# Two seven-product steps in each of four pairs of up chunks of a fused two-block transformer kernel

## The chip, the cores and the metric

The kernel runs on one core of a Trainium2 chip. The metric is the device time of one execution in microseconds, the median of the runs shown. Engines are named as the profile does: PE (matrix products; PEld its weight loads), DVE (VectorE), ACT (ScalarE), POOL (GpSimd), SP (SyncE, which issues the loads of the weights).

## What is computed

Two transformer blocks follow each other on 256 tokens of width 2048, in float32. The part that matters here is the feed-forward network of the second block:

```python
h = rmsnorm_2(x, g_ffn[l])
u = causal_dwconv(h @ w_up[l], ffn_conv_w[l]) + ffn_conv_b[l]
gate, val = jnp.split(u, 2, axis=-1)
x = x + (jax.nn.silu(gate) * val) @ w_down[l]
```

`w_up` is 2048 x 11264: the *second up product*. Its result goes through a causal convolution of three taps along the tokens, then SiLU and a product, and becomes the operand of the down product.

## The kernel before

**Granules.** Every weight matrix streams through the core once, as granules of 512 KB: two tiles of 128 rows by 512 columns (one granule is [128, 1024]). SP loads a granule into one of four `raw` slots (`load_granule`, L869). ACT rounds it to `wh` (L938), DVE subtracts `wl = raw - wh` (L1296, "the remainder"), and PE multiplies: for two tiles and two halves of the tokens the three products x_hi*w_hi, x_hi*w_lo and x_lo*w_hi, 12 matmuls of 512 columns (L1882). `wh` and `wl` have four slots too: ACT rounds granule i once PE is done with granule i-4, and SP loads granule i once the remainder of i-4 is taken.

**Chunks.** 512 output columns are a chunk: eight granules for an operand of 2048 rows, gathered in two PSUM banks (256 tokens are two banks). The second up product has 22 chunks, 0 to 21, and 176 granules. Chunks 0 and 1 are interleaved; the others follow each other, in banks 0-1 and 2-3 in turn.

**The order of work.** A plan is made first: a list of rows, one row per granule. Row s holds granule s's rounding and remainder, the load of granule s+4, whatever was booked for row s with `later(row, ...)`, and PE's multiplication of granule s-3. Each engine walks this one list in order and takes its own entries; semaphores tie them together. So a late entry holds up all that stands behind it on its engine.

**What follows an up chunk.** `plan_up(n)` (L537) is called at row s = last granule + 4 (plus a lateness of 0, 4 and 2 rows for chunks 0, 1 and 2), and books:

| row | entry | engine, line |
|---|---|---|
| s | `up_rows`: scale the two banks into `ST` | ACT L1216, L1217 |
| s+1 | `turn`: transpose in 32x32 blocks; `leave`: write to DRAM | DVE L1413, L1415; POOL L1830 |
| s+3 | `bring`: four reads back | POOL L1838 |
| s+9 | `up_keep` | ACT L1224, L1225 |
| s+10 | `up_first`: first tap, four pieces | ACT L1232 |
| s+11 | `up_second`: four pieces, each after its piece of `up_first` | DVE L1743 |
| s+12 | `up_third` | DVE L1750, L1753 |
| s+13 | `up_silu` | ACT L1236 |
| s+14 | `up_gated`, then `act2_hi` | DVE L1757, ACT L1240 |
| s+15 | `act2_lo` | DVE L1761 |

`up_first` of a chunk waits for `act2_lo` of the one before. The banks of a chunk are free for the chunk after next once `up_rows` has read them.

**Seven-product steps.** The first up product ("gated": chunk pairs 1 to 10) and the first chunks of the two down products hold some steps by Strassen's scheme (in Winograd's form). There two chunks run side by side (`product_side_by_side`, L323): granules of both alternate, and two granules of the same weight rows (one for each chunk) make a *unit*, a 2x2 block of tiles against a 2x2 block of the operand. It takes 7 x 3 = 21 matmuls in place of 24: `multiply_base` (9) and `multiply_forms` (12). Four shared banks, those that the chunks themselves do not use, gather the products that go into several outputs. In row u+1 of a unit u stand:

```python
do("base_hi", s - 1)
do("sums", s - 1)
do("base_lo", s - 1)
do("forms_hi", s - 1)
do("forms_lo", s - 1)
```

`base_hi` is ACT L958, `sums` DVE L1324, L1327, L1329, `base_lo` DVE L1310 (it frees both raw slots), `forms_hi` ACT L964, `forms_lo` DVE L1333. PE's two entries stand in row u+4. The first `multiply_base` of a pair waits until the banks that become the shared ones are drained. Five rows after the last unit `shared_out` copies the shared banks out (ACT L980, four copies), then `shared_sums` (DVE L1369, L1371) and `shared_last` (DVE L1376, L1378) in a row each; `shared_bank` (DVE L1399, L1400 for the first chunk of a pair, L1404 for the second) adds them onto the chunk's banks. Sums of the operand that units need are made once per stage (`xs_sum`, `xs_hi`, `xs_lo`).

In the gated stage a pair's two units are its fourth and sixth step, and what follows a pair is little: one transposition for two chunks and no convolution. The second up product has no unit.

Of the kernel before, what the change touches and what calls it, by code (L numbers as in the profile page):

```python
# [8 lines left out]
P = 128  # L9
# [11 lines left out]
ALU = mybir.AluOpType  # L21
# [76 lines left out]
def two_block_kernel(nc, t, out):  # L98
    with ExitStack() as ctx:
# [127 lines left out]
        tile_sums = tmp.rearrange("p (k c) -> p k c", k=4)  # L227
# [4 lines left out]
        xs_in, gated_in = (view(n, [P, 2, 4, P], o) for n, o in (("xs_in", o_a), ("gated_in", o_b + 32 * K)))  # L232
        xs_out, gated_out = (view(n, [P, 2, 4, P], o) for n, o in (("xs_out", o_a + 4 * K), ("gated_out", o_b + 36 * K)))
# [45 lines left out]
        seven_operand = {"gated": "ffn", "out1": "act1", "down": "act2"}  # L279
        side_by_side = {"gated": {}, "out1": {}, "down": {}}  # L280
# [7 lines left out]
        def do(name, *args):  # L288
            plan[-1].append((name, args))
# [193 lines left out]
        def plan_gated(n):  # L483
            def after(s, chunk):
                chunk.drained = [("silu", n), ("gated", n)]
                if n // 2 in GATED_PAIRS:
                    do("shared_bank", n)
# [12 lines left out]
            return after  # L500
# [178 lines left out]
        for n in range(2, 22):  # L679
            last_up = product(t["w_up2"], "N", "ffn2", PAIRS16, ("up", n), plan_up(n), n)  # L680
# [79 lines left out]
        def gated_at(n):  # L760

            return at("shared_bank", n) if n // 2 in GATED_PAIRS else product_of("gated", n)
# [54 lines left out]
        bases = {"gated": (gated_hi, gated_lo), "out1": (base_hi, base_lo), "down": (base_hi, base_lo)}  # L817
        x_places = {"gated": (gated_in, gated_out), "out1": (xs_in, xs_out), "down": (xs_in, xs_out)}
# [98 lines left out]
        def scalar(e):  # L917
# [8 lines left out]
            for name, args in phases:  # L926
# [32 lines left out]
                elif name == "forms_hi":  # L959
# [3 lines left out]
                    e.wait_ge(*at("sums", i))  # L963
                    e.copy(two_slots(wh, i), tile_sums.rearrange("p k c -> p (k c)")).then_inc(done[name], 1)  # L964
                elif name == "xs_hi":
                    stage, j = args
                    e.wait_ge(*at("xs_sum", stage, j))
                    if stage == "gated":
                        e.copy(gated_xs_hi[:], gated_out[:]).then_inc(done[name], 1)
                        continue  # L970
                    e.copy(seven_tiles(operands[seven_operand[stage]][0], stage, j)[:, :, 1], xs_out[:, :, 0])
                    e.copy(xs_hi[:, 2 * j:2 * j + 2], xs_out[:, :, 1:4]).then_inc(done[name], 1)
                elif name == "shared_out":
# [5 lines left out]
                    for k, place in enumerate((0, 3, 2, 1)):  # L979
                        e.copy(tile_sums[:, place, :], ps[:, pair.shared + k, :]).then_inc(done[name], 1)  # L980
# [228 lines left out]
                elif name == "up_rows":  # L1209
# [5 lines left out]
                    e.wait_ge(*product_of("up", n))  # L1215
# [51 lines left out]
        def vector(e):  # L1267
# [22 lines left out]
            for name, args in phases:  # L1290
# [20 lines left out]
                elif name == "sums":  # L1311
                    i, = args
                    unit = seven[i]
                    b12, b11, b22, b21 = (two_slots(raw, i)[:, 512 * k:512 * k + 512] for k in range(4))
# [15 lines left out]
                elif name == "forms_lo":  # L1330
                    i, = args
                    e.wait_ge(*at("forms_hi", i))
                    e.tensor_tensor(two_slots(wl, i), tile_sums.rearrange("p k c -> p (k c)"), two_slots(wh, i).bitcast(F32),  # L1333
                                    ALU.subtract).then_inc(done[name], 1)
                elif name == "xs_sum":
# [3 lines left out]
                    if j > 0:  # L1339
                        e.wait_ge(*at("xs_lo", stage, j - 1))  # L1340
                    elif stage != "gated":

                        e.wait_ge(*through(last_ffn if stage == "out1" else last_up))
# [9 lines left out]
                elif name == "xs_lo":  # L1353
                    stage, j = args
                    e.wait_ge(*at("xs_hi", stage, j))
                    if stage == "gated":
                        e.tensor_tensor(gated_xs_lo[:], gated_out[:], gated_xs_hi[:].bitcast(F32),
                                        ALU.subtract).then_inc(done[name], 1)
                        continue
                    hi, lo = (seven_tiles(x, stage, j)[:, :, 1] for x in operands[seven_operand[stage]])  # L1360
# [3 lines left out]
                elif name == "shared_sums":  # L1364

                    stage, q = args
                    p1, p7, p6, _ = (tile_sums[:, k, :] for k in range(4))
# [4 lines left out]
                elif name == "shared_last":  # L1372
                    stage, q = args
                    _, second, first, p5 = (tile_sums[:, k, :] for k in range(4))
# [4 lines left out]
                elif name == "shared_first":  # L1379
# [5 lines left out]
                    e.tensor_tensor(X[:, 0, n0], X[:, 0, n0], tile_sums[:, 0, :], ALU.add)  # L1385
                    e.tensor_tensor(X[:, 1, n0], X[:, 1, n0], tile_sums[:, 1, :], ALU.subtract).then_inc(done[name], 1)
                elif name == "shared_second":
# [4 lines left out]
                    e.tensor_tensor(X[:, :, n1], X[:, :, n1], tile_sums[:, 2:4, :], ALU.add).then_inc(done[name], 1)  # L1392
                elif name == "shared_bank":
                    n, = args
                    bank0, bank1 = banks(named["gated", n])
                    e.wait_ge(*product_of("gated", n))
                    if n % 2 == 0:
                        e.wait_ge(*at("shared_sums", "gated", n // 2))
                        e.tensor_tensor(bank0, bank0, tile_sums[:, 0, :], ALU.add)  # L1399
                        e.tensor_tensor(bank1, bank1, tile_sums[:, 1, :], ALU.subtract).then_inc(done[name], 1)  # L1400
                    else:
                        b = named["gated", n].bank
                        e.wait_ge(*at("shared_last", "gated", n // 2))
# [786 lines left out]
```

## Time and profile before

| | |
|---|---|
| time, median of 3 runs | 2405.98 us (2405.49 to 2408.77) |
| time of the profiled execution | 2406.82 us |
| its span | 2404.6 us |
| PE busy | 2392.5 us (99%) |
| DVE busy | 1749.4 us (73%) |
| ACT busy | 1351.1 us (56%) |
| DMA, mean | 229 GB/s |
| granted TensorE clock | 0.999 of full |

The span is that of the traced instructions; the time also has what lies before and after them. The profile gives for each group of instructions its busy time and the mean length of one; a timeline gives start and length of single ones, and in brackets how long the engine stood idle before it and whose end released it. Two instructions on one engine overlap by some 0.1 us at their ends, so the distance between their starts is what one costs its engine, and the length is what one waiting for it sees.

### The profile page before, as it was taken

The page shows a single profiled execution, that of the slowest core. Times are in us where ns is not written, and L with a number is a line of the kernel's source. Part 1 is how long each engine was busy: PE and PEld are TensorE (multiplying, and loading weights), DVE is VectorE, ACT ScalarE, POOL GpSimd, SP SyncE. Part 2 cuts the span into 40 slices and gives each one's busy share as a digit, 9 for nine tenths or more (in the row PEclk, how much of TensorE's full clock was granted, in tenths as well). Part 3 has the DMA queues.
Part 4 walks back from the last instruction along what each step waited for, and adds up shares of the span by engine and source line. Part 5 has one row for each costly group of instructions (what it writes and reads, how often), then busy time and mean ns, then how long its engine had stood idle before and what let it go on. Part 6 is the DMA issues. An engine that isn't in the chain of part 4 may idle for free.

```text
span 2404.6 us, 28035 instructions
## 1 busy us (share of the span) xinstructions
PE 2392.5 (99%) x10606; PEld 1980.5 (82%) x10606; DVE 1749.4 (73%) x2148; ACT 1351.1 (56%) x1649; POOL 190.6 (8%) x351
## 2 busy tenths in 40 slices
PE   9999999999999999999999999999999999999998
PEld 7888888888888888888888888888888888888887
DVE  7575555666778888889786865786577766678886
ACT  7554565445555555555555754544566666665554
POOL 0000000001000000000001100111111111110000
PEclk9999999999999999999999999999999999999999
DMA  8777655778866767776678777887788888886664
GB/s 275 225 221 232 193 192 184 215 238 246 259 218 221 229 222 222 226 235 229 195 227 274 246 235 220 256 245 236 235 244 249 241 244 241 242 241 206 219 215 160
DMA packets 155734, 550.06 MB, mean 229 GB/s; under 512 B 20176, under 2 KB 20688, under 8 KB 155216
## 3 DMA queue, kind: packets, MB, share of 16 engines
q1 hardware_dynamic: 131552, 470.91, 62.0%
q0 software_dynamic: 23472, 76.57, 11.6%
q8 instruction: 84, 1.38, 0.2%
q10 hardware_dynamic: 576, 0.79, 0.1%
q14 instruction: 50, 0.41, 0.1%
HBM read 507.82 MB, written 40.37 MB: 228 GB/s over the span
## 4 chain that ended last, share of the span: by engine, by line
PE 93%; DVE 4%; DMA 1%; ACT 1%; issue 1%; SPq 0%; ACTq 0%; DVEq 0%
PE ps L1882 92%; DVE wl L1296 1%; DMA raw<-in_w_ffn_in 1%; DMA raw<-in_w_in 0%; DMA raw<-in_w_ffn_out 0%; ACT wh L938 0%; DVE wl L1333 0%; DVE tmp L1324 0%; ACT wh L964 0%; PE ps L2020 0%; DVE tmp L1327 0%; ACT tmp L980 0%; DVE tmp L1329 0%; PE ps L2040 0%; DVE xs_in L1345 0%
## 5 line engine op out<-in xcount | busy, mean ns | idle before, releaser
L1296 DVE TENSOR_TENSOR wl<-raw,wh 128x1024 fp32r<-128x1024 f32 x786 | 954.3, 1221 | 590.1 <-ACT wh L938 589.2
L938 ACT CAST wh<-raw 128x1024 fp32r<-128x1024 f32 x786 | 820.3, 1049 | 731.4 <-PE ps L1882 702.4
L1882 PE MATMUL ps<-wh,x4g_hi 128*128 128x512 f32 x704 | 273.9, 389 | 0.0
L1882 PE MATMUL ps<-wl,x4g_hi 128*128 128x512 f32 x704 | 273.9, 389 | 0.0
L1882 PE MATMUL ps<-wh,x4g_lo 128*128 128x512 f32 x704 | 273.9, 389 | 0.0
L1882 PE MATMUL ps<-wh,h_hi 128*128 128x512 f32 x576 | 224.4, 392 | 2.0 <-DVE wl L1296 1.3
L1882 PE MATMUL ps<-wh,h_lo 128*128 128x512 f32 x576 | 223.0, 389 | 0.0
L1882 PE MATMUL ps<-wl,h_hi 128*128 128x512 f32 x576 | 222.8, 389 | 0.0
L1882 PE MATMUL ps<-wh,x1g_hi 128*128 128x512 f32 x564 | 219.4, 389 | 0.0
L1882 PE MATMUL ps<-wl,x1g_hi 128*128 128x512 f32 x564 | 219.4, 389 | 0.0
L1882 PE MATMUL ps<-wh,x1g_lo 128*128 128x512 f32 x564 | 219.4, 389 | 0.0
L1882 PE MATMUL ps<-wh,act_hi 128*128 128x512 f32 x560 | 218.0, 389 | 0.0
L1882 PE MATMUL ps<-wl,act_hi 128*128 128x512 f32 x560 | 217.9, 389 | 0.0
L1882 PE MATMUL ps<-wh,act_lo 128*128 128x512 f32 x560 | 217.9, 389 | 0.0
L1838 POOL DMA_DIRECT2D Z<-rows x268 | 146.2, 552 | 351.2 <-DMA rows<-Y 338.4
L1830 POOL DMA_DIRECT2D rows<-Y x67 | 37.5, 560 | 1607.0 <-DVE Y L1415 1607.0
L1882 PEld LDWEIGHTS ps<-wh,x4g_lo 128*128 128x128 f32 x704 | 132.1, 188 | 27.6
L1882 PEld LDWEIGHTS ps<-wh,x4g_hi 128*128 128x128 f32 x704 | 132.1, 188 | 27.4
L1882 PEld LDWEIGHTS ps<-wl,x4g_hi 128*128 128x128 f32 x704 | 132.1, 188 | 27.4
L964 ACT CAST wh<-tmp 128x2048 fp32r<-128x2048 f32 x44 | 84.3, 1915 | 89.4 <-DVE tmp L1329 84.4
L1882 PEld LDWEIGHTS ps<-wh,h_hi 128*128 128x128 f32 x576 | 108.0, 188 | 24.9 <-issue 2.1
L1882 PEld LDWEIGHTS ps<-wh,h_lo 128*128 128x128 f32 x576 | 108.1, 188 | 22.7
(384 smaller groups left out, 4067.0 us busy)
## 6 DMA issues: line engine op xcount, KB each, us to landing
raw<-in_w_in SPq DMA_DIRECT2D x196, 512.0 KB, 4.3
raw<-in_w_ffn_in SPq DMA_DIRECT2D x176, 512.0 KB, 4.3
raw<-in_w_up SPq DMA_DIRECT2D x176, 512.0 KB, 4.7
raw<-in_w_ffn_out SPq DMA_DIRECT2D x88, 512.0 KB, 4.3
raw<-in_w_down SPq DMA_DIRECT2D x88, 512.0 KB, 4.3
rows<-Y POOLq DMA_DIRECT2D x67, 512.0 KB, 5.3
Z<-rows POOLq DMA_DIRECT2D x268, 128.0 KB, 5.1
raw<-in_w_o SPq DMA_DIRECT2D x32, 512.0 KB, 4.4
```

Source lines behind the costliest of these rows:

```text
L938: e.copy(wh[:, i % RING, :], raw[:, slot, :]).then_inc(rounded, 1)
L964: e.copy(two_slots(wh, i), tile_sums.rearrange("p k c -> p (k c)")).then_inc(done[name], 1)
L1296: e.tensor_tensor(wl[:, r, :], raw[:, i % RAW, :], wh[:, r, :].bitcast(F32), ALU.subtract).then_inc(remainder, 1)
L1830: e.dma_start(rows_out[n % 2], Y[:]).then_inc(rows_left[n % 2], 16)
L1838: e.dma_start(ZA[32 * q:32 * q + 32], rows_out[n % 2, :, 256 * q:256 * q + 256].rearrange("(a i) e -> i a e", a=4)).then_inc(rows_back[n % ...
L1882: return e.matmul(dst, weights, x, start=start, stop=stop, skip_group_check=True)
```

## The change

Chunks 2-3, 6-7, 10-11 and 14-15 of the second up product (pairs q = 1, 3, 5 and 7) run side by side in banks 4 to 7, with banks 0 to 3 as shared ones. Their steps come in the order 0, 1, 4, 2, 6 for both chunks, then 3, 5, 7 for the first and 3, 5, 7 for the second; steps 4 and 6 are units. The other chunks stay as they are. The sums of weight tiles lie in a buffer of their own (`up_sums`), beside other views that hold the rounded parts. Entries of row positions: `shared_bank` stands at s for the first chunk of such a pair and at s+2 for the second; `up_late` gives the lateness of the entries of `plan_up`: 0 and 4 rows for chunks 0 and 1, 1 and 4 rows for the chunks of such a pair, 2 rows for the first chunk after one, and 0 for all others. So the chunks in front of a pair have no lateness. `up_rows` of a side-by-side chunk waits for `shared_bank`; the first plain chunks after a pair wait for `shared_out` instead of `up_rows`. The weights of those steps are laid out on the host in the units' order.

```diff
-SEVEN = {"gated": (4, 6), "out1": (8, 10, 12, 14, 16, 18), "down": (8, 10, 12, 14, 16, 18)}
+SEVEN = {"gated": (4, 6), "up": (4, 6), "out1": (8, 10, 12, 14, 16, 18), "down": (8, 10, 12, 14, 16, 18)}
 GATED_PAIRS = range(1, 11)
 GATED_ORDER = (0, 1, 2, 4, 3, 6, 5, 7)
+UP_PAIRS = (1, 3, 5, 7)
+UP_ORDER = (0, 1, 4, 2, 6, 3, 5, 7)
...
-        tile_sums = tmp.rearrange("p (k c) -> p k c", k=4)
+        up_hi = view("up_hi", [P, 3, 512], o_b + 28 * K, FR)
+        up_lo = view("up_lo", [P, 3, 512], o_b + 74 * K, FR)
+        up_sums = view("up_sums", [P, 4, 512], o_b + 80 * K)
+        up_xs_hi = view("up_xs_hi", [P, 2, 4, P], o_b + 34 * K, FR)
+        up_xs_lo = [view(f"up_xs_lo{i}", [P, 4, P], o_b + at * K, FR) for i, at in enumerate((38, 72))]
+        tile_sums_of = {stage: up_sums if stage == "up" else tmp.rearrange("p (k c) -> p k c", k=4)
+                        for stage in ("gated", "out1", "up", "down")}
...
+        def up_late(n):
+
+            if n < 2:
+                return (0, 4)[n]
+            if n // 2 in UP_PAIRS:
+                return (1, 4)[n % 2]
+            return 2 * (n // 2 - 1 in UP_PAIRS and n % 2 == 0)
+
         def plan_up(n):
             def after(s, chunk):
                 chunk.drained = [("up_rows", n)]
-                s += (0, 4, 2)[n] if n < 3 else 0
+                if n // 2 in UP_PAIRS:
+                    later(s + n % 2 * 2, lambda: do("shared_bank", "up", n))
+                s += up_late(n)
...
-        for n in range(2, 22):
-            last_up = product(t["w_up2"], "N", "ffn2", PAIRS16, ("up", n), plan_up(n), n)
+        plan_x_sums("up", len(granules), 0)
+        for q in range(1, 11):
+            if q in UP_PAIRS:
+                cleared = [[("pool_out", 1)], [("x_split", 1, 1)]] if q == 1 else [[("up_rows", 2 * q - 4 + n)] for n in range(2)]
+                product_side_by_side(t["w_up2"], "up", q, 4, UP_ORDER, 5, [plan_up(2 * q), plan_up(2 * q + 1)], 0, cleared,
+                                     ("shared_out", "shared_sums", "shared_last"))
+                continue
+            for n in (2 * q, 2 * q + 1):
+                last_up = product(t["w_up2"], "N", "ffn2", PAIRS16, ("up", n), plan_up(n), n)
+                if q - 1 in UP_PAIRS:
+                    last_up.cleared = [("shared_out", "up", q - 1)]
         down_from = len(granules)
         for j in range(4):
             later(down_from + 43 + j, lambda j=j: do("load_gf", j))
         plan_x_sums("down", down_from + 5, 4)
         for q in range(2):
-            cleared = ([("pool_out", 1)], [("x_split", 1, 1)]) if q == 0 else ([("shared_out", "down", 0)],) * 2
+            cleared = ([("up_rows", 14)], [("up_rows", 15)]) if q == 0 else ([("shared_out", "down", 0)],) * 2
...
+        def up_at(n):
+
+            return at("shared_bank", "up", n) if n // 2 in UP_PAIRS else product_of("up", n)
...
+            if unit.pair.stage == "up":
+                return [[x[:, n] for x in (up_xs_hi[:, unit.place], up_xs_lo[unit.place])] for n in range(4)]
...
-                    e.wait_ge(*product_of("up", n))
+                    e.wait_ge(*up_at(n))
...
+                    elif unit.pair.stage == "up":
+                        if unit.pair.q > UP_PAIRS[0]:
+                            e.wait_ge(*at("shared_bank", "up", 2 * unit.pair.q - 3))
...
+                    if stage == "up":
+                        e.tensor_tensor(up_xs_lo[0][:], up_out[:, 0], up_xs_hi[:, 0].bitcast(F32), ALU.subtract)
+                        e.tensor_tensor(up_xs_lo[1][:], up_out[:, 1], up_xs_hi[:, 1].bitcast(F32),
+                                        ALU.subtract).then_inc(done[name], 1)
...
-                    n, = args
-                    bank0, bank1 = banks(named["gated", n])
-                    e.wait_ge(*product_of("gated", n))
+                    stage, n = args
+                    tile_sums = tile_sums_of[stage]
+                    bank0, bank1 = banks(named[stage, n])
+                    e.wait_ge(*product_of(stage, n))
                     if n % 2 == 0:
-                        e.wait_ge(*at("shared_sums", "gated", n // 2))
+                        e.wait_ge(*at("shared_sums", stage, n // 2))
                         e.tensor_tensor(bank0, bank0, tile_sums[:, 0, :], ALU.add)
                         e.tensor_tensor(bank1, bank1, tile_sums[:, 1, :], ALU.subtract).then_inc(done[name], 1)
                     else:
...
-        "w_up2": stream(paired(i["w_up_2"][0])), "w_down": sevens(stream(i["w_down_2"][0]), SEVEN["down"], range(2)),
+        "w_up2": sevens(stream(paired(i["w_up_2"][0])), SEVEN["up"], UP_PAIRS), "w_down": sevens(stream(i["w_down_2"][0]), SEVEN["down"], range(2)),
```

## Rows read from the trace of the kernel before

**Rows 1.** The page: busy time, and the chain that ended last.
```profile
PE 2392.5 (99%) x10606; PEld 1980.5 (82%) x10606; DVE 1749.4 (73%) x2148; ACT 1351.1 (56%) x1649; POOL 190.6 (8%) x351
...
PE 93%; DVE 4%; DMA 1%; ACT 1%; issue 1%; SPq 0%; ACTq 0%; DVEq 0%
```

**Rows 2.** Windows, gated stage and second up product: length, busy (count), clock, DMA, GB/s.
```profile
640.00:1095.00 455.00, 454.08 (x1997) 374.12 (x1996) 384.10 (x401) 246.55 (x277) 30.75 (x56) 1.00 0.71 227
1686.70:2165.20 478.50, 478.50 (x2112) 396.21 (x2111) 330.24 (x443) 297.26 (x393) 60.30 (x110) 1.00 0.82 242
```

**Rows 3.** Waits of PE in the gated stage: waited for, us in total, times, longest.
```profile
PE ps L1882 <- DVE wl L1333: 0.5, 2, 0.3
PE ps L1882 <- DVE gated_lo L1310: 0.4, 2, 0.2
```

**Rows 4.** Timeline of ACT in the second up product.
```profile
1904.57 1.05 ACT L938 CAST wh<-raw 128x1024 fp32r<-128x1024 f32 x1 [0.93 <-PE ps L1882]
1905.52 0.68 ACT L1216 ACTIVATE tmp<-ps,small 128x512 f32<-128x512 f32 x1
1906.10 0.68 ACT L1217 ACTIVATE tmp<-ps,small 128x512 f32<-128x512 f32 x1
...
1908.24 0.61 ACT L1224 COPY FW<-Z 128x512 f32<-128x512 f32 x1
...
1910.96 2.08 ACT L1232 ACTIVATE tmp<-FW,cst 128x256 f32<-128x256 f32 x4
...
1919.56 0.63 ACT L1236 ACTIVATE tmp<-tmp 128x512 f32<-128x512 f32 x1 [0.34 <-DVE tmp L1753]
...
1923.83 0.62 ACT L1240 CAST act_hi<-tmp 128x512 fp32r<-128x512 f32 x1 [1.89 <-DVE tmp L1757]
```

**Rows 5.** Timeline of DVE in the second up product.
```profile
1909.51 0.70 DVE L1413 STREAM_TRANSPOSE Y<-tmp 128x512 f32<-128x512 f32 x1
1910.14 0.67 DVE L1415 STREAM_TRANSPOSE Y<-tmp 128x512 f32<-128x512 f32 x1
...
1915.15 1.67 DVE L1743 SCALAR_TENSOR_TENSOR tmp<-FW,cst,tmp 128x255 f32<-128x255 f32 x4
...
1917.87 1.26 DVE L1750 SCALAR_TENSOR_TENSOR tmp<-FW,cst,tmp 128x254 f32<-128x254 f32 x3
...
1919.44 1.22 DVE L1296 TENSOR_TENSOR wl<-raw,wh 128x1024 fp32r<-128x1024 f32 x1
...
1923.11 0.68 DVE L1757 TENSOR_TENSOR tmp<-tmp 128x512 f32<-128x512 f32 x1
```

**Rows 6.** Timeline of DVE and ACT at one unit of the gated stage.
```profile
942.51 1.23 DVE L1324 TENSOR_TENSOR tmp<-raw 128x1024 f32<-128x1024 f32 x1
...
945.11 1.75 DVE L1310 TENSOR_TENSOR gated_lo<-raw,gated_hi 128x1536 fp32r<-128x1536 f32 x1
945.30 1.92 ACT L964 CAST wh<-tmp 128x2048 fp32r<-128x2048 f32 x1 [3.65 <-DVE tmp L1329]
947.25 2.29 DVE L1333 TENSOR_TENSOR wl<-tmp,wh 128x2048 fp32r<-128x2048 f32 x1 [0.39 <-ACT wh L964]
```

**Rows 7.** Timeline of the shared work at the end of one gated pair.
```profile
923.40 2.03 ACT L980 COPY tmp<-ps 128x512 f32<-128x512 f32 x4
...
927.55 0.68 DVE L1369 TENSOR_TENSOR tmp<-tmp 128x512 f32<-128x512 f32 x1
928.27 0.69 DVE L1371 TENSOR_TENSOR tmp<-tmp 128x512 f32<-128x512 f32 x1
...
936.01 1.22 DVE L1404 TENSOR_TENSOR ps<-ps,tmp 128x1024 f32<-128x1024 f32 x1
```

**Rows 8.** DMA issues in 1900 to 2000: queue, count, size, median us to landing.
```profile
raw<-in_w_up SPq DMA_DIRECT2D x37, 512.0 KB, 4.8
```

**Rows 9.** Longest wait of PE in the trace, and the window around it (as rows 2).
```profile
18.30 0.47 PE L1882 MATMUL ps<-wh,h_hi 128*128 128x512 f32 x1 [1.33 <-DVE wl L1296]
...
18.00:40.00 22.00, 21.67 (x96) 17.73 (x97) 18.73 (x28) 15.65 (x19) 0.00 (x0) 1.00 0.87 279
```

More of the change, by code:

```diff
@@ L278, in two_block_kernel @@
         seven = {}
-        seven_operand = {"gated": "ffn", "out1": "act1", "down": "act2"}
-        side_by_side = {"gated": {}, "out1": {}, "down": {}}
+        seven_operand = {"gated": "ffn", "out1": "act1", "up": "ffn2", "down": "act2"}
+        side_by_side = {"gated": {}, "out1": {}, "up": {}, "down": {}}
         onto_rows = ("shared_out", "shared_sums", "shared_first", "shared_last", "shared_second")
@@ L486, in after @@
                 if n // 2 in GATED_PAIRS:
-                    do("shared_bank", n)
+                    do("shared_bank", "gated", n)
                     later(s + 1, lambda: do("silu", n))
@@ L760, in gated_at @@
         def gated_at(n):
-            return at("shared_bank", n) if n // 2 in GATED_PAIRS else product_of("gated", n)
+            return at("shared_bank", "gated", n) if n // 2 in GATED_PAIRS else product_of("gated", n)
+        def up_at(n):
+            return at("shared_bank", "up", n) if n // 2 in UP_PAIRS else product_of("up", n)
         def product_of(*key):
@@ L815, in two_slots @@
             return x[:, i % RING:i % RING + 2, :].rearrange("p r c -> p (r c)")
-        bases = {"gated": (gated_hi, gated_lo), "out1": (base_hi, base_lo), "down": (base_hi, base_lo)}
-        x_places = {"gated": (gated_in, gated_out), "out1": (xs_in, xs_out), "down": (xs_in, xs_out)}
+        bases = {"gated": (gated_hi, gated_lo), "out1": (base_hi, base_lo), "up": (up_hi, up_lo),
+                 "down": (base_hi, base_lo)}
+        x_places = {"gated": (gated_in, gated_out), "out1": (xs_in, xs_out), "up": (up_in, up_out),
+                    "down": (xs_in, xs_out)}
         def all_three(x):
@@ L963, in scalar @@
                     e.wait_ge(*at("sums", i))
+                    tile_sums = tile_sums_of[seven[i].pair.stage]
                     e.copy(two_slots(wh, i), tile_sums.rearrange("p k c -> p (k c)")).then_inc(done[name], 1)
@@ L967, in scalar @@
                     e.wait_ge(*at("xs_sum", stage, j))
-                    if stage == "gated":
-                        e.copy(gated_xs_hi[:], gated_out[:]).then_inc(done[name], 1)
+                    if stage in ("gated", "up"):
+                        x_hi = gated_xs_hi if stage == "gated" else up_xs_hi
+                        e.copy(x_hi[:], x_places[stage][1][:]).then_inc(done[name], 1)
                         continue
@@ L979, in scalar @@
                     for k, place in enumerate((0, 3, 2, 1)):
-                        e.copy(tile_sums[:, place, :], ps[:, pair.shared + k, :]).then_inc(done[name], 1)
+                        e.copy(tile_sums_of[stage][:, place, :], ps[:, pair.shared + k, :]).then_inc(done[name], 1)
                 elif name == "first_hi":
@@ L1313, in vector @@
                     unit = seven[i]
+                    tile_sums = tile_sums_of[unit.pair.stage]
                     b12, b11, b22, b21 = (two_slots(raw, i)[:, 512 * k:512 * k + 512] for k in range(4))
@@ L1332, in vector @@
                     e.wait_ge(*at("forms_hi", i))
+                    tile_sums = tile_sums_of[seven[i].pair.stage]
                     e.tensor_tensor(two_slots(wl, i), tile_sums.rearrange("p k c -> p (k c)"), two_slots(wh, i).bitcast(F32),
@@ L1340, in vector @@
                         e.wait_ge(*at("xs_lo", stage, j - 1))
+                    elif stage == "up":
+                        e.wait_ge(*product_of("out2", 3))
                     elif stage != "gated":
@@ L1366, in vector @@
                     stage, q = args
-                    p1, p7, p6, _ = (tile_sums[:, k, :] for k in range(4))
+                    p1, p7, p6, _ = (tile_sums_of[stage][:, k, :] for k in range(4))
                     e.wait_ge(*at("shared_out", stage, q))
@@ L1373, in vector @@
                     stage, q = args
-                    _, second, first, p5 = (tile_sums[:, k, :] for k in range(4))
+                    _, second, first, p5 = (tile_sums_of[stage][:, k, :] for k in range(4))
                     e.wait_ge(*at("shared_sums", stage, q))
@@ L1384, in vector @@
                     e.wait_ge(*at("shared_sums", stage, q))
-                    e.tensor_tensor(X[:, 0, n0], X[:, 0, n0], tile_sums[:, 0, :], ALU.add)
-                    e.tensor_tensor(X[:, 1, n0], X[:, 1, n0], tile_sums[:, 1, :], ALU.subtract).then_inc(done[name], 1)
+                    e.tensor_tensor(X[:, 0, n0], X[:, 0, n0], tile_sums_of[stage][:, 0, :], ALU.add)
+                    e.tensor_tensor(X[:, 1, n0], X[:, 1, n0], tile_sums_of[stage][:, 1, :], ALU.subtract).then_inc(done[name], 1)
                 elif name == "shared_second":
@@ L1401, in vector @@
                     else:
-                        b = named["gated", n].bank
-                        e.wait_ge(*at("shared_last", "gated", n // 2))
+                        b = named[stage, n].bank
+                        e.wait_ge(*at("shared_last", stage, n // 2))
                         e.tensor_tensor(ps[:, b:b + 2, :], ps[:, b:b + 2, :], tile_sums[:, 2:4, :], ALU.add).then_inc(done[name], 1)
```

9 lines of the change are left out of this document (6 added, 3 removed).

## The prediction

> **What bounds the kernel now.** I read the page first: PE is busy for 2392.5 of 2404.6 us and makes up 93% of the chain that ended last, while DVE has 73% and ACT 56% [rows 1]. So PE's matmuls are the time, unless something makes PE wait. Then the windows of the two stages to be compared: in the second up product PE is busy for the whole 478.50 us with 2112 matmuls, 0.2266 us each, so 2.72 us a granule (12 matmuls) and no wait at all; DVE is busy for 69% of it and ACT for 62% [rows 2]. In the gated stage, which has units already, DVE is busy for 84%, and PE waited 0.9 us in all over its 20 units [rows 2, 3]. The reader should see that DVE and ACT have room on average in both. But the timeline shows that they don't run free: ACT stood 1.89 us before `act2_hi`, waiting for DVE, and 0.34 us before the SiLU [rows 4]. Each such wait also holds up the roundings behind it. The question is therefore what the longest chain through ACT and DVE is, from one point to the next that PE waits for, against PE's own pace.
>
> The executions shown have a median of 2405.98; the profiled one took 2406.82, and the sum is made against that.
>
> **What PE saves.** Eight units, each 21 matmuls in place of 24: 24 x 0.2266 = **-5.4 us**. Nothing else can be gained, since PE has no wait in the stage.
>
> **The opening of the first pair.** Call the plan rows of a pair 0 to 15 by its granules; its units are 4-5 and 8-9. The first `multiply_base` waits for `up_rows` of the chunk before the pair. For q = 1 this is chunk 1, whose lateness of 4 puts `up_rows` at row 7, behind the rounding of granule 7, which itself waits for granule 3's multiplication. PE comes to the unit right after granule 3. So it waits for the end of a matmul (0.16 us after the next could start, at a length of 0.39), a rounding 0.95 and two scalings 1.26 [rows 4], with two handovers of 0.03 to 0.1: **2.5 us**, with hardly a way round it: only the 0.95 of the rounding could go, if ACT were through with granule 7 early, but that rounding waits for the same matmul. Behind the wait on PE stand only its own matmuls, and DVE and ACT gain a lead meanwhile.
>
> **What a unit asks.** On DVE the sums take 2.60 (942.51 to 945.11), `base_lo` 1.75, and `forms_lo` 2.29, which starts 0.39 later, since `forms_hi` needs 1.92 on ACT after the sums: 7.0 us from the first to the last [rows 6], against 2 x 1.14 for two remainders. The up stage also has, per chunk, `up_second` 1.58 and `up_third` 1.57, a turn of 1.30, `up_gated` 0.6 and `act2_lo`, of the same size, 0.6 [rows 5]. With `up_rows` 6 rows apart after a pair, these entries fall on the next pair's units. For q = 3, 5, 7 row by row: row 3 `up_third` of the chunk 2q-3; row 4 a turn; row 5 unit, then `up_gated` and `act2_hi`; row 6 `act2_lo`, `up_keep`; row 7 `up_first`; row 8 `up_second`; row 9 unit, `up_third`, SiLU; row 11 `up_gated`, `act2_hi`; row 12 `up_keep`; row 13 `shared_out`, `up_first`; row 14 `shared_sums`, `up_second`; row 15 `shared_last`, `up_third`; row 16 `shared_bank`; row 17 `up_gated`, `act2_hi`, `up_rows`; row 18 `act2_lo`, a turn.
>
> **Chain A, unit to unit.** From the end of the first unit's `forms_lo`: `up_gated` 0.68, `act2_hi` 0.52, rounding 0.95, `up_keep` 1.04 (two copies of 0.52), rounding 0.95, `up_first` 2.08, last piece of `up_second` 0.40, sums 2.60, `base_lo` 1.75 = 10.97 [rows 4 to 6]. PE meanwhile has the first unit's forms and granules 6 and 7: 3 x 2.72 = 8.16. PE waits **2.8 us** if that `forms_lo` came just in time. How early can it come? From the end of granule -1: rounding, remainder (2.3), `up_third` 1.57, turn 1.30, sums 2.60, forms 4.2 = 12.0, where PE needs it after 4 x 2.72 + 2.04 = 12.9. So at most 0.9 less, and the wait is 1.9 at the least: already more than the pair saves (1.36). I take 2.9 with the handovers, since DVE enters row 3 behind `up_second` in row 2.
>
> **Chain B.** The second unit's forms: sums, then `forms_hi` 1.92 and `forms_lo` 2.29 against `base_lo` 1.75 and nine matmuls 2.04: 0.42, with handovers **0.5 us**. The gated stage paid 0.26 there when its base was late [rows 3].
>
> **Chain C, the tail of the pair.** From the second `forms_lo`: `up_third` 1.65, SiLU 0.54, rounding 1.08, remainder 1.14, `up_gated` 0.68, `act2_hi` 0.52, rounding 0.95, `up_keep` 1.04, rounding 0.95, `shared_out` 1.93 (four copies), `up_first` 1.98, rounding 1.08, remainder 1.22 = 14.8 [rows 4, 5, 7]; PE has forms and granules 10 to 13, 13.6: waits 1.2. Behind ACT's four copies and `up_first` in row 13 stand the roundings of granules 14 and on, whose slots have long been free. Then DVE alone: remainder 1.14, `shared_sums` 1.33, `up_second` 1.58 = 4.05 in a row of 2.72 (+1.3); the same with `shared_last` and `up_third` (+1.3); row 16 with `shared_bank` 1.2 gives back 0.4; row 17 `up_gated`, `act2_hi`, `up_rows` 1.16, rounding, remainder = 4.7, less 2.72 and 0.4 (+1.6); row 18 `act2_lo`, turn, remainder 3.1 (+0.3). Sum **5.8 us**.
>
> So a pair costs 2.9 + 0.5 + 5.8 = 9.2, three pairs 27.6. For q = 1 the chunks before stand elsewhere and only the last rows crowd: 0.9, beside the 2.5. Between the pairs plain rows let DVE and ACT catch up, so nothing carries over.
>
> **Other parts.** The operand sums (`xs_*`, about 3 us of DVE once, estimated as one unit's sums) come where DVE has room: nothing. Traffic is the same; POOL's entries only change rows, and a bring waits for `up_keep` of the chunk before, which stands in its own row. The loads for a second unit start at the first's `base_lo` and land in 4.8 us [rows 8], two at once in an estimated 7.0 (another 512 KB at the stage's 242 GB/s is 2.2) [rows 2, 8]; chain A takes 9.2 up to those sums, so they are covered. In rows 19 and on a late remainder makes late loads: between 0 and 5 us over all; I take 1.4. If chains A and C were not there this cover would go too.
>
> Sum: -5.4 + 2.5 + 0.9 + 27.6 + 1.4 = **+27.0**, so 2433.8 against 2406.8, and 2433 against the median.
>
> **The page that says otherwise.** DVE and ACT are busy for 69% and 62% of the stage [rows 2], and a pair adds to DVE 2 x (6.5 - 2.3) for its units, 2.7 for `shared_sums` and `shared_last` and 2.4 for `shared_bank`, 13.5 us, so 54 in all: (330 + 54) of 478 is 80%, less than the gated stage's 84%. The Trainium skill (Perfetto Trace Analysis, "Identifying the Most-Contended Engine") says to take the engine with the highest occupancy and improve that one first; by it the time would be 2403.5, the first rival. The gated stage's rows agree with it [rows 2, 3]. Its section "Optimization Strategy" asks for what blocks that engine in its own regime, which is what I did.
>
> **Rivals.**
> - *Only PE's work counts: not slower.* The lead of DVE and ACT hides the chains, as in the gated stage, where 20 units cost 0.9 [rows 3]: 0.4 for eight, and the opening 2.5: -5.4 + 2.9 = -2.5, 2403.5. It decides from the point where `forms_lo` of the first unit comes 2.8 us ahead of PE; my count gives 0.9 at the most. For it speaks the average room. Even so it is within 0.2%. 8%.
> - *Only the units cost.* Chain C is taken by the lead; A at its least 1.9: 3 x 2.4 + 2.5 - 5.4 = +4.3 up to +9, 2411 to 2416. 12%.
> - *More than I count.* Late loads cost their 5 us, or the clock falls. The trace held 1.00 through the 1.33 us wait at 18.3 us [rows 9]; here are three waits of about 2.5. If one granule ran at half rate, 1.2 in place of 2.4 GHz, after each of the three waits, that adds 3 x 2.72 = 8: 2441; late loads at their upper end add 3.6: 2437. 10%. The Trainium skill (TensorE: Matmul & The Clock Gate, "HAM oscillation — how this bites in real kernels") says that an array which waits on data again and again runs at the low clock; no wait as long as these is in this trace to test it.
> - That the matmuls don't go away can't be: the plan counts 21 for each unit.
>
> **The numbers.** My forecast has 70%: 2433, by itself 2424 to 2442. The range 2413 to 2446 takes in the second rival's upper part and most of the third. A change of under 0.2% (4.8 us) can't be told from none here. Slower holds the forecast, the third rival and most of the second; same the first and the rest; faster by over 4.8 would need all of the 5.4.
>
> **What would show it.** In the profile after: 24 fewer matmuls; PE waiting for `up_rows` (ACT L1216, L1217) once, 2.5 us; for the base remainder 2 to 3 us once in each of three pairs; for remainders (L1296) at rows 14 to 18; the same pattern at q = 3, 5, 7, weaker at q = 1; the clock at 1.00. No waits of PE in rows 13 to 18 would prove chain C wrong, no wait at the second unit chain A.

## The result and the profile after

| | before | after |
|---|---|---|
| time, median of 4 runs | 2407.38 us | 2435.66 us (2434.59 to 2437.05) |
| time of the profiled execution | 2406.82 us | 2436.11 us |
| ratio of the times | | 1.012 (1.0105 to 1.0135) |

The changed kernel is 28.3 us slower; the profiled executions differ by 29.3. Forecast were +27.0 us, 2433, and a range of 2413 to 2446.

The page of the changed kernel, busy time and the chain that ended last (answers to [rows 1]):

```profile
PE 2402.1 (99%) x10582; PEld 1980.0 (81%) x10582; DVE 1803.5 (74%) x2206; ACT 1364.2 (56%) x1666; POOL 190.6 (8%) x351
...
PE 80%; DVE 11%; ACT 5%; DMA 2%; issue 2%; SPq 0%; ACTq 0%; DVEq 0%
```

PE has 24 matmuls fewer (10582 for 10606) and yet is busy longer: its records run from start to end of pipelined matmuls, and some are stretched, as the last section shows. The tell-tale is the chain: PE had 93% of it and has 80%, and DVE and ACT together went from 5% to 16%.

The stage in one window (answers to the second of [rows 2]), 30.0 us longer:

```profile
1686.70:2195.20 508.50, 486.99 (x2090) 394.23 (x2089) 384.72 (x502) 310.52 (x411) 60.28 (x110) 0.99 0.76 228
```

PE's waits in the stage, by what it waited for: us in total, times, longest (before, there were none):

```profile
PE ps L1935 <- DVE wl L1335: 11.7, 13, 1.2
PE ps L1935 <- DVE up_lo L1349: 6.8, 4, 2.2
PE ps L1935 <- ACT tmp L1256: 2.4, 1, 2.4
PE ps L1935 <- DVE wl L1377: 0.5, 2, 0.3
```

So 21 us are waits that the profile attributes: one for `up_rows` (ACT L1256, the opening), four for base remainders (L1349), three of them of about 2.2 at the second units of q = 3, 5 and 7, two for the forms of first units (L1377), and thirteen for plain remainders (L1335). From start to start of neighbouring matmuls, each less the usual 0.2266, the stage lost 24.9 us in 21 waits (by this measure a wait is some 0.16 longer than the idle time in the profile, since the record of the matmul before it runs on for that long after the next could have started) and 9.3 us in matmuls that followed each other more slowly than usual. 24.9 + 9.3 less the 5.4 saved is 28.8, of 29.8 by which the stage grew from its first to its last matmul.

The third pair (q = 5), its units four granules apart. Timeline of ACT, DVE and PE of the changed kernel from the first unit's `forms_lo` to the second unit's base (left out: the second `up_keep` copy, `act2_lo`, two remainders, `up_second`, two sums and PE's other matmuls):

```profile
1927.63 2.29 DVE L1377 TENSOR_TENSOR wl<-up_sums,wh 128x2048 fp32r<-128x2048 f32 x1 [0.38 <-ACT wh L1002]
1929.84 0.68 DVE L1810 TENSOR_TENSOR tmp<-tmp 128x512 f32<-128x512 f32 x1
1930.56 0.62 ACT L1279 CAST act_hi<-tmp 128x512 fp32r<-128x512 f32 x1 [2.96 <-DVE tmp L1810]
1931.08 1.05 ACT L975 CAST wh<-raw 128x1024 fp32r<-128x1024 f32 x1
1932.04 0.61 ACT L1263 COPY FW<-Z 128x512 f32<-128x512 f32 x1
...
1933.07 1.04 ACT L975 CAST wh<-raw 128x1024 fp32r<-128x1024 f32 x1
...
1934.03 2.08 ACT L1271 ACTIVATE tmp<-FW,cst 128x256 f32<-128x256 f32 x4
...
1936.87 1.22 DVE L1367 TENSOR_TENSOR up_sums<-raw 128x1024 f32<-128x1024 f32 x1
...
1939.46 1.75 DVE L1349 TENSOR_TENSOR up_lo<-raw,up_hi 128x1536 fp32r<-128x1536 f32 x1
...
1941.36 0.47 PE L1935 MATMUL ps<-up_hi,x4g_hi 128*128 128x512 f32 x1 [2.18 <-DVE up_lo L1349]
```

This is chain A, link by link: with `up_second` (1935.29 to 1936.96) and the other sums between, one link follows the other without a pause, across two engines, from 1929.84 to 1941.21. One link is another than the prediction had: it let the chain go through the four pieces of `up_first`, which end at 1936.11, and the last piece of `up_second`; here the remainder in front (L1335, 1934.15 to 1935.38) and all four pieces of `up_second` on DVE end 0.4 later than that way would. The reader should see that neither engine is overloaded here: ACT stood idle for 2.96 us in front of `act2_hi`, with two roundings behind it.

The tail of the same pair, chain C, in the same kernel:

```profile
1952.42 2.03 ACT L1019 COPY up_sums<-ps 128x512 f32<-128x512 f32 x4
1954.33 2.09 ACT L1271 ACTIVATE tmp<-FW,cst 128x256 f32<-128x256 f32 x4
...
1957.38 1.23 DVE L1335 TENSOR_TENSOR wl<-raw,wh 128x1024 fp32r<-128x1024 f32 x1 [3.60 <-ACT wh L975]
1958.53 0.69 DVE L1421 TENSOR_TENSOR up_sums<-up_sums 128x512 f32<-128x512 f32 x1
...
1959.86 1.66 DVE L1796 SCALAR_TENSOR_TENSOR tmp<-FW,cst,tmp 128x255 f32<-128x255 f32 x4
1961.43 1.22 DVE L1335 TENSOR_TENSOR wl<-raw,wh 128x1024 fp32r<-128x1024 f32 x1
...
1962.71 0.50 PE L1935 MATMUL ps<-wh,x4g_hi 128*128 128x512 f32 x1 [1.03 <-DVE wl L1335]
```

ACT makes four copies and four taps before it rounds granule 14; DVE waits 3.60 us for that, and then has 4.05 us of work (1957.38 to 1961.43) in a row that PE does in 2.72. The PE line is granule 15.

### The profile page after: what moved, and what is told of

Read it like the earlier page. It is cut to its first block, busy times and chain, and to the rows that moved or that the text cites. A ratio compares the mean times of both kernels' runs of the same rounds, so it can differ in the third digit from the quotient of the medians.

```text
span 2434.3 us, 28095 instructions
## 1 busy us (share of the span) xinstructions
PE 2402.1 (99%) x10582; PEld 1980.0 (81%) x10582; DVE 1803.5 (74%) x2206; ACT 1364.2 (56%) x1666; POOL 190.6 (8%) x351
## 4 chain that ended last, share of the span: by engine, by line
PE 80%; DVE 11%; ACT 5%; DMA 2%; issue 2%; SPq 0%; ACTq 0%; DVEq 0%
PE ps L1935 79%; DVE wl L1335 3%; ACT wh L975 2%; DVE tmp L1796 1%; DVE wl L1377 1%; DMA raw<-in_w_ffn_in 1%; ACT wh L1002 1%; DVE tmp L1803 1%; ACT tmp L1271 1%; DMA raw<-in_w_up 1%; DMA raw<-in_w_ple_gate 0%; DVE tmp L1367 0%; DMA raw<-in_w_down 0%; DVE Y L1468 0%; DVE up_sums L1367 0%
## 5 line engine op out<-in xcount | busy, mean ns | idle before, releaser
L1335 DVE TENSOR_TENSOR wl<-raw,wh 128x1024 fp32r<-128x1024 f32 x770 | 934.1, 1221 | 559.3 <-ACT wh L975 557.9
L975 ACT CAST wh<-raw 128x1024 fp32r<-128x1024 f32 x770 | 801.4, 1049 | 678.3 <-PE ps L1935 625.6
L1935 PE MATMUL ps<-wh,x4g_hi 128*128 128x512 f32 x648 | 254.2, 392 | 11.7 <-DVE wl L1335 11.7
L1935 PE MATMUL ps<-wl,x4g_hi 128*128 128x512 f32 x648 | 252.3, 389 | 0.0
L1935 PE MATMUL ps<-wh,x4g_lo 128*128 128x512 f32 x648 | 252.2, 389 | 0.0
L1935 PEld LDWEIGHTS ps<-wh,x4g_hi 128*128 128x128 f32 x648 | 121.6, 188 | 43.5 <-DVE wl L1335 14.3
L1935 PEld LDWEIGHTS ps<-wh,x4g_lo 128*128 128x128 f32 x648 | 121.6, 188 | 25.7
L1935 PEld LDWEIGHTS ps<-wl,x4g_hi 128*128 128x128 f32 x648 | 121.7, 188 | 24.7
```

The costliest lines, as they stand in the source:

```text
L975: e.copy(wh[:, i % RING, :], raw[:, slot, :]).then_inc(rounded, 1)
L1335: e.tensor_tensor(wl[:, r, :], raw[:, i % RAW, :], wh[:, r, :].bitcast(F32), ALU.subtract).then_inc(remainder, 1)
L1935: return e.matmul(dst, weights, x, start=start, stop=stop, skip_group_check=True)
```

## Experiments

Three explanations were held against each other. The **order theory** is the prediction's: chains of entries through ACT and DVE, made by the order of the plan. The **load theory**: DVE has too much work in a pair. The **DMA theory**: weights land late. Each ratio is to the kernel before, in runs beside it, with its 95% interval.

**e1, the same work in closer rows.** All entries of `plan_up` stay, in other rows:

```diff
-                    later(s + 10 + i - (i > 4), lambda name=name: do(name, n))
+                    later(s + 10 + (0, 0, 1, 2, 2, 3, 3)[i], lambda name=name: do(name, n))
```

> The changed kernel with the entries behind an up chunk drawn closer: up_second in the row of up_first, up_third one row earlier, SiLU with up_gated one row earlier in one row, act2_hi and act2_lo together. Same instructions, same amount of work on each engine. Order theory (the loss comes from the chains through ACT and DVE that the order of the entries makes): chains A and C lose several hops, because up_second no longer stands in front of the second unit's sums and up_gated and act2_hi no longer straddle the first unit's; nearly the whole loss goes, the opening wait of 2.5 us at the first pair and its slow matmuls (1.6) stay: 5 to 8 us over the kernel before, about 2413. Load theory (DVE has too much work in a pair, in any order): as the changed kernel, about 2435. DMA theory (late loads): as the changed kernel.

Measured: 2414.34 against 2408.12, ratio 1.0025 (1.0016 to 1.0035), +6.2 us. PE's waits:

```profile
PE ps L1935 <- DVE up_lo L1349: 4.0, 3, 1.3
PE ps L1935 <- ACT tmp L1256: 2.4, 1, 2.4
PE ps L1935 <- DVE wl L1377: 0.8, 3, 0.3
PE ps L1935 <- DVE wl L1335: 0.2, 1, 0.2
```

Not one instruction was taken away, and 22 of 28 us are gone. DVE was busy for 386.8 us in the stage, as much as in the changed kernel (384.7): that rules out the load theory as the main cause.

**e2, and other latenesses.** On top of e1:

```diff
             if n < 2:
-                return (0, 4)[n]
+                return (0, 3)[n]
             if n // 2 in UP_PAIRS:
-                return (1, 4)[n % 2]
-            return 2 * (n // 2 - 1 in UP_PAIRS and n % 2 == 0)
+                return (1, 3)[n % 2]
+            return 3 * (n // 2 - 1 in UP_PAIRS)
```

> As e1, with other latenesses: 3 rows for chunk 1, 1 and 3 rows for the chunks of a pair, 3 for both chunks behind a pair. Order theory: PE waits only at the opening, some 1.5 us (up_rows of chunk 1 stands a row earlier there), so 5.4 saved less 1.5: 3 to 4 us faster than the kernel before, about 2403.5, and the clock stays full. Load theory: about 2435, as the changed kernel.

Measured: 2403.93 against 2408.12, ratio 0.9979 (0.9970 to 0.9988): 4.2 us *faster* than the kernel before. One wait is left in the stage, and DVE is as busy as in the changed kernel (387.23 us in a window that is 30 us shorter; columns as in [rows 2]):

```profile
PE ps L1935 <- ACT tmp L1256: 0.9, 1, 0.9
```

```profile
1686.70:2165.20 478.50, 477.57 (x2105) 394.28 (x2104) 387.23 (x504) 315.62 (x411) 61.45 (x113) 1.00 0.79 245
```

The units' saving of 5.4 us was there all along. This version beats both kernels.

**e3, `act2_hi` one row later.**

```diff
-                    later(s + 10 + i - (i > 4), lambda name=name: do(name, n))
+                    later(s + 10 + i - (i > 5), lambda name=name: do(name, n))
```

> The changed kernel with one entry per chunk moved by one row: act2_hi stands in the row behind up_gated, in front of act2_lo. Order theory: ACT no longer stands idle until DVE has done up_gated before it can round the next granule, so chain A is shorter by about 1.7 us and chain C by as much at each of its two such places; about half of the loss goes: 12 to 15 us over the kernel before, about 2420. Load theory and DMA theory: no difference to the changed kernel.

Measured: 2421.69 against 2408.12, ratio 1.0056 (1.0042 to 1.0070), +13.6. PE's two largest groups of waits:

```profile
PE ps L1935 <- DVE wl L1335: 6.3, 6, 1.1
PE ps L1935 <- DVE up_lo L1349: 5.4, 3, 2.0
```

One entry per chunk, moved by one row, was half of the loss: it is the entry on ACT that waits for DVE with roundings behind it. In the profiled execution no matmuls ran slowly after the opening, which is 1.6 us of the difference; the rest is in both chains (table below).

**e4, the control.** The kernel before with e1's rows.

```diff
-                    later(s + 10 + i - (i > 4), lambda name=name: do(name, n))
+                    later(s + 10 + (0, 0, 1, 2, 2, 3, 3)[i], lambda name=name: do(name, n))
```

> The kernel before with the entries drawn closer as in e1. Order theory: PE has no wait in the up stage to lose, so no difference to the kernel before within 2 us. If the closer entries made work cheaper in themselves it would be faster.

Measured: ratio 0.9999 (0.9990 to 1.0008). The closer rows gain nothing where PE has no wait.

**e5, the first pair alone.**

```diff
-UP_PAIRS = (1, 3, 5, 7)
+UP_PAIRS = (1,)
```

> The changed kernel with UP_PAIRS = (1,): only chunks 2 and 3 side by side, two units, everything else plain. Order theory: in front of the first pair no chunk of another pair leaves its entries among the units, so chains A and C don't form; 2.5 us for the opening, 1.6 of slow matmuls after it, 0.8 at the end of the pair, less 1.4 saved: 3 to 4 us over the kernel before, about 2411. Load theory (each pair has too much DVE work): a quarter of the whole loss, 7 us over.

Measured: 2409.01 against 2406.24, ratio 1.0012 (1.0003 to 1.0021), +2.8. PE's waits:

```profile
PE ps L1935 <- ACT tmp L1256: 2.4, 1, 2.4
PE ps L1935 <- DVE wl L1335: 0.6, 1, 0.6
```

A pair with no pair before it makes two waits, the opening and one at its end. So the units alone do not make chains A and C; it takes the entries of the chunks in front, which stand elsewhere at q = 1 than at q = 3, 5 and 7. The expected 3 to 4 us lie within the interval (0.7 to 5.1), the 7 of the load theory do not. In the profiled execution no slow matmuls followed the opening.

**e6, the taps nearly left out.** Second and third tap over 8 columns (three such lines, for `up_second` and `up_third`):

```diff
-                        e.scalar_tensor_tensor(TC[:, c, 1:], f[:, c, 0:T - 1], gain("fconv", 88 + 4 * n + c), TC[:, c, 1:],
+                        e.scalar_tensor_tensor(TC[:, c, 1:9], f[:, c, 0:8], gain("fconv", 88 + 4 * n + c), TC[:, c, 1:9],
```

> The changed kernel with the second and third tap of the convolution taken over 8 columns in place of 255 and 254, so most of that part of the computation is left out; all instructions and waits stay. DVE has some 60 us less work in the stage. Order theory: chain C loses up_second and up_third, chain A keeps its hops through ACT and loses only the wait before the first unit, the opening stays: 6 to 9 us over the kernel before, about 2415. Load theory: DVE then has less work than in the kernel before, so all but the opening goes: 2 us under it to 1 over.

Measured: 2418.33 against 2406.24, ratio 1.0052 (1.0036 to 1.0067), +12.1, more than either theory said. PE's waits:

```profile
PE ps L1935 <- DVE up_lo L1349: 3.7, 3, 1.6
PE ps L1935 <- DVE wl L1335: 3.5, 3, 1.2
PE ps L1935 <- ACT tmp L1256: 2.4, 1, 2.4
PE ps L1935 <- DVE wl L1377: 0.8, 3, 0.3
```

The order theory's expectation was low by 3 us. The second units' base waits fell from 2.2 to between 0.9 and 1.6 and did not go: a part of chain A ran through `up_second`, what is left runs through ACT and the sums. Slow matmuls cost 1.6 after the opening. For the load theory the miss is 11 us, but its premise did not hold: the short taps took 38 us off DVE and not 60, so DVE was busy for 346.2 us in the stage, less than in the changed kernel (384.7) and still more than in the kernel before (330.2). What this run shows is that with less work on DVE by a tenth PE was kept waiting; the load theory falls by e1 and e2.

**e7, half the bytes.** In `load_granule`:

```diff
+                if granules[i][2] == "ffn2":
+                    e.dma_start(raw[:, slot, 0:512], src[:, 0:512]).then_inc(landed[slot], 16)
+                    return
                 e.dma_start(raw[:, slot, :], src).then_inc(landed[slot], 16)
```

> The changed kernel with half of each granule of the second up product loaded, 256 KB in place of 512 (the other half of the slot is what it held before, so the product is another one); all instructions and waits stay. DMA theory (late loads make part of the loss): the loads land in some 3 in place of 4.8 us and most of the loss goes. Order theory: PE waits for entries on DVE and ACT whose weights landed long before, so it stays within 3 us of the changed kernel, about 2433 to 2436.

Measured: 2432.93, ratio 1.0113 (1.0099 to 1.0127). The loads landed in 2.7 us in place of 4.7, and PE's waits stayed nearly as they were. DMA issues of 1900 to 2000 us (the changed kernel, then this one), and the two largest groups of waits:

```profile
raw<-in_w_up SPq DMA_DIRECT2D x34, 512.0 KB, 4.7
raw<-in_w_up SPq DMA_DIRECT2D x34, 256.0 KB, 2.7
```

```profile
PE ps L1938 <- DVE wl L1338: 12.6, 15, 1.2
PE ps L1938 <- DVE up_lo L1352: 6.5, 3, 2.2
```

The DMA theory falls as the main cause. The interval overlaps with the changed kernel's, so the 1.4 us that the prediction gave to late loads are not shown. They are not ruled out either. In rows 19 and 20, where late loads were to begin, PE lost 0.3 to 0.4 us a pair in both kernels. But ACT waited for landings 14 times in the stage of the changed kernel, 29.8 us, nearly all of it just behind a pair, and 3 times, 10.5 us, in this one; and in the profiled executions PE lost 3.0 us less here, all of it from the start of a first unit to that of the second. So late loads behind one pair may have taken the lead away that the next one needed. That isn't shown: e10, with full loads, lost only 3.1 there at q = 5 and 7, where the changed kernel lost 4.2 and 3.5 and this one 2.8.

**e8, the opening alone.** e2 with chunk 1 a row later again:

```diff
-                return (0, 3)[n]
+                return (0, 4)[n]
```

> The kernel of e2 with the lateness of chunk 1 back at 4 in place of 3, nothing else. Order theory: the one wait at the opening grows from about 1.1 to 2.5 us, and after it the clock falls for some nine matmuls, as it did in the changed kernel after waits of over 2 us and not after those of 1.3: 1.4 for the wait and 1.6 for the clock, 2.5 to 3 us slower than e2, about 1.2 faster than the kernel before. If the clock has to do with the pairs and not with the wait: 1.4 slower than e2.

Measured: 2404.04 against 2406.24, ratio 0.9992 (0.9983 to 1.0000), against e2's 0.9979: about 3 us slower by the ratios, 2 by the medians, with overlapping intervals. The wait was there as expected, 2.4 us. In its profiled execution the clock did *not* fall (last section), so the price of the clock isn't shown by this pair.

**e9, two rows of lateness for the chunk in front of a pair.**

```diff
-            return 2 * (n // 2 - 1 in UP_PAIRS and n % 2 == 0)
+            return 2 * (n // 2 - 1 in UP_PAIRS)
```

> The changed kernel with one lateness undone: the second chunk behind a pair, which stands in front of the next, has 2 rows again in place of 0. Order theory: its later entries leave rows 13 to 18, so chain C goes, and chain A is down to about 0.9; but its up_rows now stands in row 5, behind the first unit's roundings, and the first multiply_base waits for it, about 4 us in each of three pairs, with slow matmuls behind it at times: 15 to 20 us over the kernel before, about 2424, and PE's longest wait is on ACT (up_rows), four times. Load theory and DMA theory: as the changed kernel.

Measured: 2422.46 against 2405.7, ratio 1.0063 (1.0046 to 1.0080), +16.8. PE's waits:

```profile
PE ps L1935 <- ACT tmp L1256: 13.9, 4, 4.3
PE ps L1935 <- DVE wl L1335: 0.6, 1, 0.6
```

One cause was exchanged for another: chain C is gone, no second unit waits, and three more waits for `up_rows` take their place. So a chunk without lateness in front of a pair avoids waits of up to 4.3 us at the opening, and chains A and C are the price.

**e10, `shared_out` one row later.**

```diff
-                later(pair.units[-1].i + 5 + k, lambda name=name: do(name, stage, q))
+                later(pair.units[-1].i + 5 + (stage == "up") + k, lambda name=name: do(name, stage, q))
```

> The changed kernel with shared_out, shared_sums and shared_last of the up pairs one row later, so that shared_out no longer stands in row 13 in front of up_first. Order theory: chain C gets shorter but not away, since the same work now falls on rows 14 to 16: the waits at its start fall from 1.2 each to 0.7 and 0.9 and those after stay: 4 to 6 us faster than the changed kernel, about 2430; the waits at the second unit stay at 2.2. If shared_out is the cause of chain C by itself: 11 us faster.

Measured: 2431.71 against 2405.7, ratio 1.0103 (1.0087 to 1.0118), +26.0, where the changed kernel has +28.3. That is 2.3 us less by the medians and 4 by the ratios, where 4 to 6 were expected, with intervals that overlap. The waits at the second units stayed at 2.2, and the remainders' fell from 11.7 to 9.4 us. In the trace chain C got 1.8 us shorter in each of three pairs (4.4 for 6.2 from the second unit to granule 20), with a longer last wait (1.7 for 1.3), and the end of the first pair got 1.9 longer. The four copies are a link of chain C, not its cause.

## Why the prediction was right

The terms were held against PE's starts: what each stretch took, less 0.2266 us for each matmul in it. The first row runs from the last matmul in front of the first unit to the first of the second unit, the next from there to the first matmul of granule 20; three numbers are q = 3, 5 and 7. The last two rows are the same two stretches at q = 1. All of it is from the profiled executions.

| stretch | forecast | changed kernel | e7 | e3 | e1 |
|---|---|---|---|---|---|
| up to the second unit (chain A) | 2.9 | 3.9, 4.2, 3.5 | 2.8, 2.8, 2.8 | 2.8, 1.9, 1.9 | 1.6, 1.6, 1.6 |
| from there to granule 20 (chains B and C) | 6.3 | 6.2, 6.2, 6.2 | 6.2, 6.2, 6.2 | 3.6, 3.6, 3.6 | 1.3, 1.3, 1.2 |
| q = 1: opening | 2.5 | 4.29 | 4.28 | 2.65 | 4.26 |
| q = 1: the pair's end | 0.9 | 0.95 | 0.95 | 0.07 | 0.01 |

The numbers of the changed kernel add up to 35.3 us, of 35.4 in its whole stage; less the 5.4 saved and the 0.1 that the stage lost before, that is the growth of 29.8.

- **The saving, -5.4.** 24 matmuls fewer, and e2 shows it: 4.2 us faster with one wait of 1.1 left.
- **The opening, 2.5.** One wait on `up_rows`, 2.40 by the profile and 2.56 from start to start. The chunk that stands in front of the first pair, chunk 1, is the one such chunk that has a lateness; with three rows in place of four (e2) the wait is 1.1. The other 1.6 of the table are slow matmuls behind the wait, which the sum had not.
- **Chain A, 2.9 a pair.** The mechanism was right, the size too small by about 1 a pair. The wait at the second unit was 2.3, and 0.6 at granule 6 belongs to the same chain: 0.61 + 2.34 = 2.95 at q = 5. What the sum lacked stands in front of it. The sum took the first unit's `forms_lo` to come just in time, with a lead of 0.9 at the most, and it came late: PE waited 0.42 for the base there at q = 5 and 0.43 for the forms at q = 3 and 5, and the first matmul after each of these waits was followed some 0.1 late too. Why it was late stays open; late loads behind the pair before, from which the prediction had nothing carry over, are one candidate (e7). The chain itself is shown by the timeline above and by e1, e2 and e3, which shorten or break it.
- **Chains B and C, 0.5 and 5.8.** 6.2 measured in each pair. By single waits it looks like less, 1.19 + 1.27 + 1.33 = 3.8 at q = 5, and no wait for forms at the second unit: the slow matmuls there filled the first 1.5 us of what PE would have waited. Where the clock held (e7, q = 3) the waits are 0.43 for the forms, then 0.99 + 1.15 + 1.26 + 1.29 = 4.7, and the stretch takes the same 6.2.
- **First pair's end, 0.9.** One wait of 0.78, 0.95 with the slower start behind it.
- **Late loads, 1.4.** Not shown and not ruled out (e7).
- **The clock, 1.00 by the prediction's signs.** That sign failed: it was 0.99 in the stage and 0.50 in stretches of it. A fall of the clock was a part of the third rival, which gave it 8 us. It cost 1.6 at the opening, where only PE's own work stood behind the wait, and nothing at the second units, where ACT and DVE set the pace anyway.
- **The total.** The stage grew by 29.8, 2.8 more than the sum: +1.8 at the opening, +2.8 in chain A, -0.4 in B and C, -1.4 for late loads, whose share, if any, is within the chains. So the order of the entries explains most of the loss by itself. That the total is as near as it is owes something to luck: the 1.4 for late loads stood in for the 1.6 of a clock that the sum held at full.
- **The rivals.** "Only PE's work counts" fell: the lead in front of the first unit was no 0.9, since PE waited up to 0.43 for its forms. The rule of the Trainium skill (Perfetto Trace Analysis, "Identifying the Most-Contended Engine") pointed to PE, and its occupancy stayed at 99% while the kernel got slower; that section adds that the busy share of matmuls is no good measure of how much TensorE has left, and names among others that of the weight loads, which was 82% before and 81% after. What decided was what the Trainium skill (Perfetto Trace Analysis, "Optimization Strategy") asks for, what blocks that engine in its own stretch. The section "HAM oscillation — how this bites in real kernels" (the Trainium skill, TensorE: Matmul & The Clock Gate), of which the trace before had shown nothing, was borne out in part: PE did drop to 1.2 GHz after waits on data. But the section tells it of longer waits, after each of which the array starts cold; here it came after waits of 2.3 to 2.6 us too, in some executions and not in others, and passed after 7 to 11 matmuls.

## What to carry to other kernels

An engine at 99% can be held up by two at 56% and 74%, if these walk one list in order: add up the longest chain of entries from one point that the busy engine needs to the next, and hold it against that engine's own pace, rather than the loads. An entry that waits for another engine (`act2_hi`) belongs a row behind the one that feeds it, and a new step must be placed together with the entries that fall on its rows: here the same change with other rows went from 28 us slower to 4 faster. And where such a chain sets the pace, a slower TensorE cost nothing. Two pairs that follow each other closely have to be looked at together; the first one alone cost 3 us.

## What was not expected of the hardware

After most of the long waits the matmuls ran at half rate. PE in the changed kernel at the second unit of q = 5 (start, length); spacing goes from 0.32 to 0.43 us, where 0.2266 is usual, and 0.427 is 512 columns at 1.2 GHz:

```profile
1941.67 0.53 PE L1935 MATMUL ps<-up_lo,x4g_hi 128*128 128x512 f32 x1
1941.99 0.63 PE L1935 MATMUL ps<-up_hi,x4g_lo 128*128 128x512 f32 x1
1942.42 0.63 PE L1935 MATMUL ps<-up_hi,up_xs_hi 128*128 128x512 f32 x1
1942.85 0.63 PE L1935 MATMUL ps<-up_lo,up_xs_hi 128*128 128x512 f32 x1
```

The granted clock was 0.50 while that lasted, and 0.96 over the stretch around both units (columns as in [rows 2]):

```profile
1942.00:1944.50 2.50, 2.50 (x7) 2.00 (x6) 2.50 (x3) 0.50 (x1) 0.00 (x0) 0.50 0.92 279
1917.60:1961.60 44.00, 40.85 (x169) 31.98 (x167) 35.36 (x47) 26.52 (x35) 2.74 (x5) 0.96 0.66 193
```

The same opening wait in e8, after which the clock held:

```profile
1746.77 0.47 PE L1935 MATMUL ps<-up_hi,x4g_hi 128*128 128x512 f32 x1 [2.40 <-ACT tmp L1256]
1747.08 0.40 PE L1935 MATMUL ps<-up_lo,x4g_hi 128*128 128x512 f32 x1
1747.31 0.39 PE L1935 MATMUL ps<-up_hi,x4g_lo 128*128 128x512 f32 x1
```

Over the profiled executions of the changed kernel, e1, e3 and e5 to e10, PE had 21 waits in this stage of 2.30 us and more from start to start, the usual spacing taken off. After 14 of them some 7 to 11 matmuls ran at 1.2 GHz, which stretched them by 1.5 to 2.3 us; after the other 7 none was slow. After the three longest (3.60, 3.97 and 4.43, in e9) it was every time; none of the waits of up to 2.13 was followed by such a run. The same instruction after the same wait (2.56, the opening) was followed by slow matmuls in five executions and by none in four. So the same wait could have such a tail in one execution and not in another. What the tail cost depended on what stood behind it: 1.6 us at the opening, nothing at the second units, where the stretch to granule 20 lost 6.2 us with it (four times) and without (twice, in e7), and 4.4 to 4.5 in e10 with it (twice) and without (once). Why the clock fell after one and not after the other stays open. Apart from that, the first matmul after any wait is followed 0.1 us later than usual, which makes 2 us over 21 waits.
